# Attention's value product on one Trainium2 core: one fp32 matmul replaced by three products of rounded parts

## The chip, the cores and the metric

The kernel runs on one core of a Trainium2 chip. A core has five engines with a queue of their own each: TensorE (PE in the profile, PEld for its weight loads), VectorE (DVE), ScalarE (ACT), GpSimd (POOL) and SyncE (SP), which here only issues DMA transfers. Each engine takes its instructions strictly in the order in which they were written, and engines wait for one another by semaphores. The metric is the device time of one execution in microseconds (us), from the first to the last instruction. Lower is better.

## What is computed

One layer of a hybrid block over 2048 tokens of width 1024: an input projection, a sparse attention branch, an mLSTM branch, their merge, and a mixture of experts. The change lies in the attention branch, whose last lines in the reference are

```python
logits = jnp.einsum('bqgrd,bqkgd->bqgrk', q_b, k_sel).astype(jnp.float32) * att_scale
logits = jnp.where(valid[:, :, None, None, :], logits, NEG_INF)
p = jax.nn.softmax(logits, axis=-1)
return jnp.einsum('bqgrk,bqkgd->bqgrd', p.astype(v.dtype), v_sel)
```

There are 8 query heads of dimension 64 in two groups (one key and value head for each), and blocks of 128 queries. The kernel does not gather the selected keys: it adds a mask to the scores of all keys that a block may see. The mLSTM recurrence (`mlstm_chunkwise`, 4 heads of dimension 128) is independent of the attention and is computed in the same stage, in between.

## The kernel before

All that follows is about one stage, the function `attend_and_recur`. The stages ahead of it (projection and indexer) and behind it (merge, experts) are not touched.

**Steps.** The stage runs over 32 pairs (n, v), `STEPS`: n is one of 16 query blocks, v one of 2 groups. A pair has n+1 flat steps j, one for each block of 128 keys, 272 flat steps in all, numbered f. All engines walk the same list of flat steps. At each f TensorE computes the transposed scores of 128 keys and 4 heads times 128 queries into `ST` (`logits_t`, L2175 to L2177: two products in the format fp32r and one bf16 product that adds the mask), ScalarE takes the exponential into `PT`, called t_probT (L2342), and TensorE multiplies the values `V`, called t_v, with it into `O`, called t_O (`values`, L2185). This last product has plain fp32 operands. V carries a 65th column of ones, so that row 64 of t_O is the sum of the exponentials. When a pair has ended, ScalarE copies t_O out (L2334).

**The maxima.** The exponential needs each query's maximum. So TensorE also computes the untransposed scores four pairs ahead (`logits`, L2146, into t_L, a ring of 3 buffers), VectorE takes their maxima (L2370), VectorE reduces them at the end of the pair (L2375, t_neg_max), GpSimd makes four diagonal matrices of them (`diagonal`, L2087, t_diag_max), and TensorE turns these into a row (`shift_row`, L2154) that ScalarE copies beside the queries (L2273, t_q_shift).

**The other work.** `side(f)` puts pieces of other work behind the attention's at certain flat steps, on every engine. For 32 units of the causal convolution ScalarE starts (L2297), VectorE adds three taps (L2421), ScalarE takes a tanh (L2303) one flat step later, and VectorE finishes (L2429). For 16 chunks of the mLSTM, one every 15 flat steps from f = 32 on, there are small products on TensorE (t_B), and on VectorE the gates (L2438), t_m_PT, t_m_KW, t_m_Y, a long run of operations on 128x4 elements (L2467 to L2481, the end of it three Newton steps of L2478 to L2480), t_m_T (L2484) and t_m_CN (L2489). GpSimd has three multiplications for a chunk: t_m_QW (L2096), t_m_CN (L2104) and t_m_T (L2110).

**Order.** At flat step f TensorE issues `logits_t(f)`, then `values(f-1)`, then the due `logits` and `side(f)`. `logits_t(f)` waits for the exponential of f-2, since ST has two buffers. `values(f-1)` waits for the exponential of f-1.

```python
                    if before:
                        values(*before)
                    before = (s, j)
```

The ring of t_probT has 3 buffers; the exponential of f waits for `values(f-3)` (`pv_ok`).

## Time and profile before

| what | us |
|---|---|
| median of 3 runs | 3365.78 (3364.29 to 3367.91) |
| span of the profiled execution | 3365.9 |
| the stage, first transposed scores to the last copy-out | about 1204 to 1892 |
| TensorE busy in 1203 to 1893 | 617 of 690 |
| VectorE busy there | 420 |
| ScalarE busy there | 285 |
| GpSimd busy there | 145 |

A matmul's row gives its start and a modelled duration that includes the way through the array, so two rows in a row overlap; how long the array is taken by one is read from the distance of starts. A plain fp32 matmul leaves two rows. Before and behind the stage all engines meet at a barrier, so what the stage wins or loses in length the kernel wins or loses.

### The profile page before, as it was taken

To read this page: it belongs to the slowest core of one execution; us is meant where nothing else is said; L and a number is where in the kernel's file an instruction comes from. 1 tells how busy PE (TensorE), PEld (TensorE's weight loads), DVE (VectorE), ACT (ScalarE), POOL (GpSimd) and SP (SyncE) were. 2 spreads that over 40 slices of the span, in tenths; PEclk is the share of its full clock that TensorE was granted. 3 is DMA by queue.
4 is the path that set the end of the run, shared out by engine and by line. 5 is a ranking of instruction groups with operands and counts; after the bars stand their busy time and mean duration, and the time that the engine had idled before them with its cause. 6 is when DMAs were issued, how large, how long until landed. Compare 5 with 4: busy or idle time off the path is not lost. (4 is left out here: it accounts for less than half of the span.)

```text
span 3365.9 us, 44849 instructions
## 1 busy us (share of the span) xinstructions
PE 3001.8 (89%) x13008; PEld 2234.4 (66%) x13008; DVE 2484.1 (74%) x3912; ACT 1814.6 (54%) x2527; POOL 462.3 (14%) x603
## 2 busy tenths in 40 slices
PE   7998899899899967999989789998499999999990
PEld 5766778678678633555545467887388888888870
DVE  6577589899999965676663445542899999999985
ACT  5322467587678443443434333332477777777770
POOL 0211110100000042221111000000111111111115
PEclk9999999999999978999999899999699999999995
DMA  3222533233212275545423466552478879667868
GB/s 125 88 69 75 146 104 125 92 119 96 65 60 76 67 166 136 116 100 109 92 67 66 125 198 175 170 175 94 188 287 316 319 287 349 243 251 256 310 246 340
DMA packets 382434, 545.93 MB, mean 162 GB/s; under 512 B 36624, under 2 KB 217536, under 8 KB 382160
## 3 DMA queue, kind: packets, MB, share of 16 engines
q1 hardware_dynamic: 349952, 434.02, 41.7%
q0 software_dynamic: 28448, 100.94, 7.9%
q10 hardware_dynamic: 3888, 9.18, 0.7%
q8 instruction: 73, 1.20, 0.1%
q14 instruction: 73, 0.60, 0.1%
HBM read 510.70 MB, written 138.19 MB: 193 GB/s over the span
## 5 line engine op out<-in xcount | busy, mean ns | idle before, releaser
L915 DVE TENSOR_TENSOR e_w_lo<-e_raw,e_w_hi 128x1024 fp32r<-128x1024 f32 x386 | 446.5, 1217 | 2.8 <-ACT e_w_hi L772 2.8
L1585 PE MATMUL x_ps<-h_hi,w_hi 128*128 128x512 f32 (+1 forms) x992 | 391.2, 394 | 5.6 <-PEq L90 4.5
L1585 PE MATMUL x_ps<-h_lo,w_hi 128*128 128x512 f32 (+1 forms) x992 | 389.1, 392 | 0.0
L1585 PE MATMUL x_ps<-h_hi,w_lo 128*128 128x512 f32 (+1 forms) x992 | 389.1, 392 | 0.0
L772 ACT CAST e_w_hi<-e_raw 128x1024 fp32r<-128x1024 f32 x386 | 377.2, 1054 | 4.9 <-PE e_pG L710 4.9
L2370 DVE CUSTOM_DVE_ANT_0 t_junk<-t_L,t_mask 128x512 bf16<-128x512 f32 (+3 forms) x320 | 185.8, 607 | 182.3 <-PE t_L L2146 181.4
L1772 DVE TENSOR_SCALAR_CACHE_REDUCE x_relu<-x_score,x_cand 128x1024 uint8<-128x1024 f32 (+3 forms) x217 | 315.6, 1486 | 3.6
L1687 ACT ACTIVATE x_relu<-x_score,x_cand 128x896 int8<-128x896 f32 (+3 forms) x217 | 281.0, 1296 | 59.8 <-DVE x_cand L1779 59.6
L2185 PE MATMUL t_O<-t_probT,t_v 128*65 128x512 f32 x544 | 292.2, 619 | 20.1 <-ACT t_probT L2342 17.7
L2342 ACT ACTIVATE t_probT<-t_ST 128x512 f32<-128x512 f32 x272 | 160.3, 593 | 276.8 <-PE t_ST L2177 276.2
L710 PE MATMUL e_pG<-e_w_hi,e_x_hi 128*128 128x512 f32 x768 | 246.7, 403 | 3.6 <-DVE e_x_lo L910 3.6
L710 PE MATMUL e_pG<-e_w_lo,e_x_hi 128*128 128x512 f32 x768 | 242.6, 397 | 0.0
L710 PE MATMUL e_pG<-e_w_hi,e_x_lo 128*128 128x512 f32 x768 | 242.1, 396 | 0.0
L2146 PE MATMUL t_L<-t_k,t_q 128*128 128x512 f32 (+3 forms) x320 | 197.1, 664 | 40.9 <-DMA t_q_shift<-q_parts 23.4
L927 DVE TENSOR_TENSOR e_w_lo<-e_raw,e_w_hi 128x1024 fp32r<-128x1024 f32 x192 | 222.4, 1220 | 11.8 <-ACT e_w_hi L785 11.8
L1585 PEld LDWEIGHTS x_ps<-h_hi,w_hi 128*128 128x128 f32 (+1 forms) x992 | 185.8, 187 | 48.3 <-issue 4.9
L1585 PEld LDWEIGHTS x_ps<-h_hi,w_lo 128*128 128x128 f32 (+1 forms) x992 | 185.6, 187 | 42.2
L1585 PEld LDWEIGHTS x_ps<-h_lo,w_hi 128*128 128x128 f32 (+1 forms) x992 | 185.9, 187 | 38.0
L785 ACT CAST e_w_hi<-e_raw 128x1024 fp32r<-128x1024 f32 x192 | 187.5, 1061 | 0.0
L1664 ACT ACTIVATE x_relu<-x_z 128x896 f32<-128x896 f32 (+5 forms) x176 | 141.4, 818 | 66.8 <-DVE x_score L1739 27.8
L710 PEld LDWEIGHTS e_pG<-e_w_lo,e_x_hi 128*128 128x128 f32 x768 | 145.4, 189 | 34.8
L710 PEld LDWEIGHTS e_pG<-e_w_hi,e_x_lo 128*128 128x128 f32 x768 | 145.2, 189 | 34.9
(417 smaller groups left out, 6285.8 us busy)
## 6 DMA issues: line engine op xcount, KB each, us to landing
e_raw<-in_w_exp_gate SPq DMA_DIRECT2D x392, 256.0 KB
e_raw<-in_w_exp_up SPq DMA_DIRECT2D x392, 256.0 KB
e_raw<-in_w_exp_down SPq DMA_DIRECT2D x192, 512.0 KB
projT<-x_out SPq DMA_DIRECT2D x120, 256.0 KB, 3.1
slot_out<-e_y POOLq DMA_DIRECT2D x48, 512.0 KB, 6.2
w_raw<-in_w_in SPq DMA_DIRECT2D x40, 512.0 KB
o_gate<-projT SPq DMA_DIRECT2D x32, 512.0 KB
slot_out<-x_zeros SPq DMA_DIRECT2D x31, 512.0 KB
```

The source lines that it names most:

```text
L710: last = nc.tensor.matmul(psG[:, q, :], x[:, k, :], w[:, k, q * DE:(q + 1) * DE], start=(k == 0 and r == 0), stop=(k == KT - 1 and r == 2))
L772: nc.scalar.copy(w_hi[:, u, :], raw[:, u, :]).then_inc(gh, 1)
L785: nc.scalar.copy(w_hi[:, KT + k, :], raw[:, KT + k, :]).then_inc(dh, 1)
L915: nc.vector.tensor_tensor(w_lo[:, u, :], raw[:, u, :], w_hi[:, u, :].bitcast(F32), ALU.subtract).then_inc(gl, 1)
L927: nc.vector.tensor_tensor(w_lo[:, KT + k, :], raw[:, KT + k, :], w_hi[:, KT + k, :].bitcast(F32), ALU.subtract).then_inc(dl, 1)
L1585: last = nc.tensor.matmul(ps[0:w, u % 4, :], wt[:, m % 2, kk, 0:w], ht[:, kk, q * 512:(q + 1) * 512], start=(kk == 0 and s == 0), stop=(kk ...
L1687: nc.scalar.activation(unused[j][:, 0:width(n)], S[:, j, 0:width(n)], ACT.Sign, bias=cand[:, j:j + 1].bitcast(F32), accum_out=cnt[:, j:j + ...
L1772: last = v.tensor_scalar(unused[j][:, 0:width(n)], S[:, j, 0:width(n)], cand[:, j:j + 1].bitcast(F32), 0.0, ALU.is_ge, ALU.add, accum_out= ...
L2146: nc.tensor.matmul(L[:, made % 3, 0:hi - lo], Q[:, n % 4, h, :], KS[:, v, lo:hi], start=True, stop=True).then_inc(l_ok, 1)
L2185: nc.tensor.matmul(O[0:AD + 1, :, :], V[:, j, v, :], PT[:, (FIRST[s] + j) % 3, :], start=(j == 0), stop=(j == n)).then_inc(pv_ok, 1)
L2342: a.activation(PT[:, f % 3, :], ST[:, u % 2, :], ACT.Exp).then_inc(p_ok, 1)
L2370: v_.tensor_tensor_reduce(junk[:, seen % 3, 0:hi - lo], L[:, seen % 3, 0:hi - lo], MB[:, n % 4, lo:hi], 1.0, -3e38, ALU.add, ALU.max, mxp[ ...
```

## The change

The values V and the exponentials PT are each split in two parts in the format fp32r: a rounded part (a copy by ScalarE, `VH` and `PH`, t_v_hi and t_probT_hi), and what is left (a subtraction, `VL` and `PL`, t_v_lo and t_probT_lo). The value product becomes VH·PH + VL·PH + VH·PL, three fp32r matmuls into the same accumulator. For the values this is done once for each quarter of the keys, by ScalarE and GpSimd. For the exponentials it is done at every flat step: ScalarE copies right behind the exponential, GpSimd subtracts at even flat steps, ahead of its `side(f)`, and VectorE at odd ones, at the start of the next flat step and ahead of that one's maxima. TensorE issues `values` two flat steps behind the scores in place of one. ScalarE's copy-out moves one flat step back. The raw values are loaded in four DMAs of their own.

```diff
@@ gpsimd
+            def probabilities_low(f):
+                pool.wait_ge(ph_ok, f + 1)
+                if f >= 3:
+                    pool.wait_ge(pv_ok, f - 2)
+                g.tensor_tensor(PL[:, f % 3, :], PT[:, f % 3, :], PH[:, f % 3, :].bitcast(F32), ALU.subtract).then_inc(ple_ok, 1)
...
                 for j in range(n + 1):
+                    if (FIRST[s] + j) % 2 == 0:
+                        probabilities_low(FIRST[s] + j)
                     side(FIRST[s] + j)
                 if s + AHEAD < len(STEPS):
                     diagonal(s + AHEAD)
@@ tensor, values
-                pe.wait_ge(p_ok, at_st[s, j] + 1)
+                f = FIRST[s] + j
+                if n == j and j % 4 == 0 and v == 0:
+                    pe.wait_ge(vl_ok, j // 4 + 1)
+                pe.wait_ge(ph_ok, f + 1)
                 if j == 0 and s:
                     pe.wait_ge(ou_ok, s)
-                nc.tensor.matmul(O[0:AD + 1, :, :], V[:, j, v, :], PT[:, (FIRST[s] + j) % 3, :], start=(j == 0), stop=(j == n)).then_inc(pv_ok, 1)
+                nc.tensor.matmul(O[0:AD + 1, :, :], VH[:, j, v, :], PH[:, f % 3, :], start=(j == 0), stop=False)
+                nc.tensor.matmul(O[0:AD, :, :], VL[:, j, v, :], PH[:, f % 3, :], start=False, stop=False)
+                pe.wait_ge(plo_ok if f % 2 else ple_ok, f // 2 + 1)
+                nc.tensor.matmul(O[0:AD + 1, :, :], VH[:, j, v, :], PL[:, f % 3, :], start=False, stop=(j == n)).then_inc(pv_ok, 1)
@@ tensor, loop
-                    if before:
-                        values(*before)
-                    before = (s, j)
+                    if len(before) == 2:
+                        values(*before.pop(0))
+                    before.append((s, j))
@@ scalar
+            def probabilities_high(s, j):
+                f = FIRST[s] + j
+                act.wait_ge(p_ok, at_st[s, j] + 1)
+                if f >= 3:
+                    act.wait_ge(pv_ok, f - 2)
+                a.copy(PH[:, f % 3, :], PT[:, f % 3, :]).then_inc(ph_ok, 1)
...
                     if f >= 3:
-                        act.wait_ge(pv_ok, f - 2)
+                        act.wait_ge(ple_ok if f % 2 else plo_ok, (f - 3) // 2 + 1)
                     a.activation(PT[:, f % 3, :], ST[:, u % 2, :], ACT.Exp).then_inc(p_ok, 1)
                     if j == 0 and s + 1 < len(STEPS):
                         shift_row(s + 1)
-                    if j == 0 and s:
-                        out(s - 1)
+                    probabilities_high(s, j)
+                    if ended(f, 1) is not None:
+                        out(ended(f, 1))
@@ vector (its probabilities_low increments plo_ok)
                 for j in range(n + 1):
+                    if FIRST[s] + j and (FIRST[s] + j) % 2 == 0:
+                        probabilities_low(FIRST[s] + j - 1)
                     while x < due(s, j):
                         maximum(s + AHEAD, x, seen)
```

Line numbers of the changed kernel differ: the value products are L2214, L2215 and L2217 there, the subtractions L2110 (GpSimd) and L2425 (VectorE), the maxima L2418.

TensorE, in the 20th pair (n = 9, v = 1), two flat steps in a row before the change:

```order
L2146 MATMUL t_L<-t_k,t_q 128x512
L2175 MATMUL t_ST<-t_q,t_k 128x512
L2176 MATMUL t_ST<-t_ident_b,t_mask 128x512
L2177 MATMUL t_ST<-t_q_shift,t_k_shift 128x512
L2185 MATMUL t_O<-t_probT,t_v 65x512
L2146 MATMUL t_L<-t_k,t_q 128x512
```

and now:

```order
L2174 MATMUL t_L<-t_k,t_q 128x512
L2201 MATMUL t_ST<-t_q,t_k 128x512
L2202 MATMUL t_ST<-t_ident_b,t_mask 128x512
L2203 MATMUL t_ST<-t_q_shift,t_k_shift 128x512
L2214 MATMUL t_O<-t_probT_hi,t_v_hi 65x512
L2215 MATMUL t_O<-t_probT_hi,t_v_lo 64x512
L2217 MATMUL t_O<-t_probT_lo,t_v_hi 65x512
L2174 MATMUL t_L<-t_k,t_q 128x512
```

The one value product has become three in the same place, and they belong to the flat step before the one that stood there.

VectorE, at flat steps 101 to 104, from t_m_T of a chunk on, before the change (the rows of 128x1 are the second half of a maximum):

```order
L2484 TENSOR_TENSOR t_m_T<-t_m_N,t_m_sc 128x512
L2370 ISA t_junk,t_max_part<-t_L,t_mask 128x512
L2370 ISA t_max_part 128x1
L2421 SCALAR_TENSOR_TENSOR t_v_Y<-t_v_U,t_v_w,t_v_Y 128x512 x3
L2489 TENSOR_TENSOR t_m_CN<-t_m_CN,t_B 128x516
L2370 ISA t_junk,t_max_part<-t_L,t_mask 128x512
L2370 ISA t_max_part 128x1
L2438 SCALAR_TENSOR_TENSOR t_m_AR<-t_m_MN,t_g_cols,t_m_caus 128x128 x4
```

and now:

```order
L2538 TENSOR_TENSOR t_m_T<-t_m_N,t_m_sc 128x512
L2425 TENSOR_TENSOR t_probT_lo<-t_probT,t_probT_hi 128x512
L2418 ISA t_junk,t_max_part<-t_L,t_mask 128x512
L2418 ISA t_max_part 128x1
L2475 SCALAR_TENSOR_TENSOR t_v_Y<-t_v_U,t_v_w,t_v_Y 128x512 x3
L2543 TENSOR_TENSOR t_m_CN<-t_m_CN,t_B 128x516
L2418 ISA t_junk,t_max_part<-t_L,t_mask 128x512
L2418 ISA t_max_part 128x1
L2492 SCALAR_TENSOR_TENSOR t_m_AR<-t_m_MN,t_g_cols,t_m_caus 128x128 x4
L2425 TENSOR_TENSOR t_probT_lo<-t_probT,t_probT_hi 128x512
```

A subtraction stands ahead of the maximum that leads to the taps, and another behind the gates.

GpSimd, around the end of a pair in the second half of the stage, before the change:

```order
L2096 TENSOR_TENSOR t_m_QW<-t_m_X,t_m_WI 128x512
L2110 TENSOR_TENSOR t_m_T<-t_m_T,t_m_gain 128x512
L2087 TENSOR_SCALAR t_diag_max<-t_ident,t_neg_max 128x128 x4
L2104 TENSOR_TENSOR t_m_CN<-t_m_CN,t_m_DEC 128x516
L2096 TENSOR_TENSOR t_m_QW<-t_m_X,t_m_WI 128x512
```

and now:

```order
L2120 TENSOR_TENSOR t_m_QW<-t_m_X,t_m_WI 128x512
L2134 TENSOR_TENSOR t_m_T<-t_m_T,t_m_gain 128x512
L2110 TENSOR_TENSOR t_probT_lo<-t_probT,t_probT_hi 128x512
L2099 TENSOR_SCALAR t_diag_max<-t_ident,t_neg_max 128x128 x4
L2110 TENSOR_TENSOR t_probT_lo<-t_probT,t_probT_hi 128x512 x4
L2128 TENSOR_TENSOR t_m_CN<-t_m_CN,t_m_DEC 128x516
```

The diagonals now have subtractions behind them that TensorE waits for two flat steps later.

## Rows read from the trace of the kernel before

**Rows 1.** Busy us by stretch: PE PEld DVE ACT POOL, granted clock, DMA

```profile
1204.00:1264.00 60.00, 52.95 (x168) 26.59 (x168) 53.66 (x162) 36.68 (x64) 28.82 (x41) 0.91 0.66 157
1264.00:1768.00 504.00, 443.26 (x1740) 243.95 (x1740) 326.17 (x948) 196.15 (x348) 98.78 (x117) 0.94 0.46 104
1768.00:1892.00 124.00, 120.19 (x498) 63.14 (x496) 39.06 (x116) 51.32 (x94) 16.07 (x16) 1.00 0.27 52
```

**Rows 2.** Waits in 1264 to 1768: us in total, times, longest us

```profile
ACT t_v_T L2303 <- DVE t_v_Y L2421: 49.6, 24, 5.1
...
PE t_ST L2175 <- ACT t_probT L2342: 18.3, 2, 14.6
PE t_O L2185 <- ACT t_probT L2342: 17.5, 10, 3.3
...
PE t_L L2146 <- DVE t_max_part L2370: 14.1, 10, 3.9
```

**Rows 3.** Timeline: start, us, instruction, [idle before]; one step, one shift_row

```profile
1701.49 1.02 PE L2185 MATMUL t_O<-t_probT,t_v 128*65 128x512 f32 x2
...
1701.92 0.19 PEld L2146 LDWEIGHTS t_L<-t_k,t_q 128*128 128x128 f32 x1 [0.29 <-issue]
1701.95 0.79 PE L2146 MATMUL t_L<-t_k,t_q 128*128 128x512 f32 x1
...
1702.58 0.40 PE L2175 MATMUL t_ST<-t_q,t_k 128*128 128x512 f32 x1
...
1511.20 0.40 PE L2154 MATMUL t_ST<-t_diag_max,t_to_row 128*128 128x512 f32 x1
...
1511.44 1.02 PE L2185 MATMUL t_O<-t_probT,t_v 128*65 128x512 f32 x2
```

**Rows 4.** Timeline of TensorE in the projection, fp32r matmuls back to back

```profile
599.80 0.39 PE L1585 MATMUL x_ps<-h_lo,w_hi 128*128 128x512 f32 x1
...
601.84 0.39 PE L1585 MATMUL x_ps<-h_lo,w_hi 128*128 128x512 f32 x1
```

**Rows 5.** Groups by line: shapes, count | busy us, mean ns | idle before

```profile
L2096 POOL TENSOR_TENSOR t_m_QW<-t_m_X,t_m_WI 128x512 f32<-128x512 f32 x16 | 20.8, 1299 | 91.1 <-DMA t_m_WI<-inter_rows 91.1
...
L924 DVE TENSOR_TENSOR e_h_lo<-e_pH,e_h_hi 128x512 fp32r<-128x512 f32 x27 | 18.7, 691 | 8.6 <-ACT e_h_hi L782 8.6
...
L782 ACT CAST e_h_hi<-e_pH 128x512 fp32r<-128x512 f32 x27 | 16.0, 592 | 0.0
```

**Rows 6.** Busy by stretch: one late stretch; sum of six; sum of three even

```profile
1487.00:1505.00 18.00, 14.45 (x55) 7.12 (x54) 15.45 (x46) 6.96 (x13) 4.43 (x6) 1.00 0.29 89
...
sum 118.00, PE 98.27 PEld 49.26 DVE 83.44 ACT 41.15 POOL 26.54; mean PE 16.38 PEld 8.21 DVE 13.91 ACT 6.86 POOL 4.42
...
sum 52.00, PE 51.29 PEld 29.95 DVE 33.98 ACT 24.57 POOL 8.63; mean PE 17.10 PEld 9.98 DVE 11.33 ACT 8.19 POOL 2.88
```

**Rows 7.** Timeline of the late stretch: GpSimd and VectorE at once, taps, tanh

```profile
1491.55 1.28 POOL L2096 TENSOR_TENSOR t_m_QW<-t_m_X,t_m_WI 128x512 f32<-128x512 f32 x1 [2.67 <-DMA t_m_WI<-inter_rows]
...
1491.59 1.25 DVE L2480 SCALAR_TENSOR_TENSOR t_m_rs<-t_m_nw,t_m_rs 128x4 f32<-128x4 f32 x1
...
1494.44 1.28 POOL L2110 TENSOR_TENSOR t_m_T<-t_m_T,t_m_gain 128x512 f32<-128x512 f32 x1 [1.61 <-DVE t_m_T L2484]
...
1494.89 2.95 DVE L2421 SCALAR_TENSOR_TENSOR t_v_Y<-t_v_U,t_v_w,t_v_Y 128x512 f32<-128x512 f32 x3
...
1497.87 0.63 ACT L2303 ACTIVATE t_v_T<-t_v_Y 128x512 f32<-128x512 f32 x1 [4.78 <-DVE t_v_Y L2421]
...
1499.04 0.64 PE L2185 MATMUL t_O<-t_probT,t_v 128*65 128x512 f32 x1 [2.77 <-ACT t_probT L2342]
```

**Rows 8.** Durations of one line each: ns min/median/max

```profile
L2480 DVE SCALAR_TENSOR_TENSOR t_m_rs<-t_m_nw,t_m_rs x48: 161/163/1253, 1331.0 to 1883.7; 128x4 f32<-128x4 f32 x48
...
L2421 DVE SCALAR_TENSOR_TENSOR t_v_Y<-t_v_U,t_v_w,t_v_Y x96: 734/752/1803, 1214.7 to 1723.0; 128x512 f32<-128x512 f32 x96
```

**Rows 9.** Timeline at the end of a pair: GpSimd, TensorE

```profile
1569.96 2.88 POOL L2087 TENSOR_SCALAR t_diag_max<-t_ident,t_neg_max 128x128 fp32r<-128x128 f32 x4 [8.66 <-DVE t_neg_max L2375]
...
1570.45 0.40 PE L2175 MATMUL t_ST<-t_q,t_k 128*128 128x512 f32 x1
```

More of the change, by code:

```diff
@@ L2261, in _ @@
                     side(FIRST[s] + j)
-            values(*before)
+            for at in before:
+                values(*at)
             for f in range(FLAT, FLAT + 20):
```

47 lines of the change are left out of this document (37 added, 10 removed).

## The prediction, made before the change was run

> **What bounds the kernel now.** I read the busy table by stretch first, to see which engine fills which part of the stage [rows 1], then the waits of the middle part [rows 2], then the timeline of an undisturbed flat step and of a disturbed one [rows 3, 7]. The stage falls into a head (1204 to 1264, some 20 flat steps, everything busy), a middle (1264 to 1768, 188 steps) and a tail (1768 to 1892, 62 steps, in which no maxima are left). In the tail TensorE is busy 120 of 124 us: it alone is the bound. In the middle it is busy 443 of 504 us and VectorE 326 of 504. TensorE's 61 us of idle time there are mostly waits on ScalarE's exponential (18.3 and 17.5) and on VectorE's maxima (14.1) [rows 2]. One of 14.6 us is a single one, at the start of the mLSTM's first chunk, and the change does not reach it. The others begin at VectorE: in the late stretch shown, the taps of a convolution unit run late, ScalarE waits 4.78 us for them with its tanh, the next exponential stands behind the tanh in ScalarE's queue, and TensorE waits 2.77 us [rows 7]. So the middle alternates. In even stretches (three that I read: 1471 to 1487, 1585 to 1604, 1663 to 1680) TensorE is busy 51.3 of 52 us. In late stretches (six: 1413 to 1431, 1449 to 1471, 1487 to 1505, 1567 to 1585, 1604 to 1626, 1643 to 1663) it is busy 98 of 118 us and VectorE sets the pace [rows 6]; the one shown has VectorE busy 15.45 of 18 us. The six hold 42 flat steps, about 7 each. They come with the run of small operations of each chunk, for 12 chunks of the middle: 84 of the 188 steps.
>
> **TensorE's part.** In an undisturbed step the value product starts at 1701.49 and the product two places on at 1702.58; between them lies one fp32r product of 512 columns [rows 3]. Nine fp32r products back to back take 601.84 - 599.80 = 2.04 us, 0.227 each [rows 4]. So the fp32 product holds the array for 1.09 - 0.227 = 0.86 us. Three fp32r products hold it for 0.68. The change saves 0.18 us for each flat step in which TensorE is the bound. In the tail that is 62 x 0.18 = 11 us, in the even steps of the middle 104 x 0.18 = 19 us: **-30**. In the head and in the late stretches I count nothing, for there TensorE waits anyway. The Trainium skill, FP8 and Floating Point Precision, section TensorE Precision Notes, says that a true fp32 product takes four passes through the array. Four times the measured 0.227 would be 0.91, the saving 0.23 a step and this term -38; the trace shows a little less than four passes, and its number is used.
>
> **ScalarE's part.** Each step gets a copy of 128x512 to fp32r, 0.59 us [rows 5], so exponential and copy take about 1.2 us. TensorE's shortest step is now 3 + 3 products of 0.227, 1.36 us. ScalarE was busy 196 of 504 us in the middle and gets 188 x 0.59 = 111 more: 307 of 504. In the tail it gets 37 on 51 of 124. It stays below the others; I cost it at nothing, and the cover is TensorE's step. If TensorE's step fell under 1.2 us plus ScalarE's side work, it would become the bound. The four copies of the values cost 4 x 0.6 us in the same cover.
>
> **VectorE's part.** One subtraction of 128x512 at every second step, 0.69 us [rows 5]. In the late stretches 84 / 2 = 42 of them, 29 us. They stand ahead of the maxima, on the chain that leads through the taps to tanh, exponential and TensorE. In the even stretches they fit in VectorE's idle time (34.0 busy of 52 us), and in the tail too (39 of 124).
>
> **GpSimd's part, first: what it does to VectorE.** A subtraction of 128x512 costs GpSimd about 1.28 us; its multiplication of that shape has a mean of 1.30 [rows 5]. The trace shows that the two engines stop each other. GpSimd's multiplication ran from 1491.55 to 1492.83, and the operation on 128x4 elements that VectorE began at 1491.59 took 1.25 us, ending with it [rows 7]; the median of that line is 0.163 [rows 8]. The three taps at 1494.89 took 2.95 us beside another one, where three times the median of 0.752 are 2.26 [rows 7, 8]: 0.69 more. So a meeting costs VectorE 0.7 to 1.1 us, say 0.9. GpSimd adds 42 subtractions in the late stretches. About half of VectorE's time there goes to operations with two inputs from SBUF (taps, gates, the small ones, the subtractions themselves), so I count half of them as meetings: 21 x 0.9 = 19 us, between 0 and 42 x 1.1 = 46. The Trainium skill, SBUF — State Buffer, section SBUF: two separate sides, says that a GpSimd operation and a VectorE operation with two SBUF inputs lock each other out for the whole instruction. By that rule the trace agrees: 1.25 us against 0.163.
>
> Together VectorE's late stretches grow by 29 + 19 = 48 us. Laid by hand over the stretch at 1487 to 1505 it comes out the same: two subtractions ahead of the taps (1.4), two meetings with GpSimd (1.4), then one more subtraction and about one meeting, 4 us in all, for 12 stretches 48. VectorE is idle for 29% of the six stretches [rows 6], mostly while TensorE catches up, so a little is absorbed where the unit falls elsewhere: **+44**.
>
> **GpSimd's part, second: its lateness.** At the end of each pair GpSimd builds four diagonals, 2.4 to 2.9 us, as soon as the maxima are there. The next even subtraction stands behind them in its queue, and TensorE wants that one 1.1 us after it has begun the scores two steps later. At 1569.96 the diagonals take 2.88 us, so the subtraction would be ready at 1572.84 + 1.28 = 1574.1, while TensorE has begun the scores in question at 1570.45 and wants it at 1571.6: 2.6 us late [rows 9]. Done so for all 28 pairs against the old times, 12 are late, 10 us in all; part of that falls together with other waits: **+8**. Behind GpSimd's subtraction its chunk multiplications are queued, and VectorE's t_m_CN waits for one of them; they come a step later than before, which the spacing of the chunk's pieces covers.
>
> **The ends.** GpSimd splits the first values between the first diagonals and the setup, 1.3 us, and behind the last exponential come a copy, a subtraction and a product in a row where one product was: **+3**.
>
> **Two steps behind.** While TensorE waits for an exponential it can now run the product of a step earlier. Ten waits at the value product, 17.5 us together [rows 2], are each cut by at most that product and the score product behind it, 0.9 us: **-9**, and the rest of each moves to the scores, which wait for the same exponential.
>
> **The sum.** -30 + 44 + 8 + 3 - 9 = +16 us on the profiled 3365.9, so 3382. The median of the runs, 3365.8, is the same number for this purpose.
>
> **Rivals.**
> (A) *TensorE stays the bound and VectorE absorbs it all.* For it: VectorE is idle for 178 of 504 us in the middle, and the additions, 65 us of subtractions there and some meetings, fit by their sum. Then 250 steps save 0.18 each, -45.5, with +8 + 3 and perhaps the -9: 3322 to 3331; where half of the late stretches absorb, up to 3359. Against it: that idle time lies mostly outside the late stretches. 33%.
> (B) *The two errors meet*, within 0.2% of now (3359 to 3372.5): 14%.
> (C) *The lock on the ports decides; slower.* Each of the 94 even subtractions in the middle meets a VectorE operation, 94 x 0.9 = 85 us. VectorE would need 326 + 65 + 85 = 476 of 504 us. TensorE now fills 88% of the middle; if VectorE can fill no more, the middle becomes 541 us, +37, less 11 in the tail, plus 11 for lateness and ends: 3403, and 3440 if the two queues of three buffers hold each other up besides. It decides from the point where VectorE needs more than 443 us, 88% of 504. By the skill's rule just named, every one of the operations can collide. 11%.
> (D) *Three products don't take less than the old one.* The third has a wait of its own ahead of it, and weight loads behind a wait show 0.29 us of idle and 0.19 us of load [rows 3], 0.48 against 0.227. Then a step costs 0.25 us more, 166 steps 41 us: 3423. Against it: the row of maxima waits too, and the value product starts 0.24 us behind it, no gap [rows 3]. 4%.
> My forecast with its neighbours (3372.5 to 3403) has 38%.
>
> **How the numbers follow.** About 0.2%, 7 us, is what a measurement of this kernel can tell from no change. Faster than that is A, 0.33; the same is B, 0.14; slower are the forecast, C and D, 0.53. The likeliest case alone runs from 3373 to 3403. The range of 8 in 10 leaves out the best part of A (below 3328) and the worst of C and D (above 3425).
>
> **What would show it.** Right: value products at a distance of 0.227 us; a tail shorter by about 11 us; VectorE's median for the subtraction near 0.69 and its mean, and that of the taps, well above their medians; more time in the waits of ScalarE's tanh on the taps; TensorE waiting at L2217 for a subtraction, at pair ends for GpSimd's. Wrong: a middle shorter than 504 us with VectorE's late stretches no longer than now (A), a distance of value products of 0.4 us (D), ScalarE as the engine waited for though not waiting itself, or a single long wait on one of the new value loads.

## The result and the profile after

The changed kernel takes 3436.03 us (median, 3432.31 to 3437.26); beside it the kernel before takes 3366.85 (3364.29 to 3369.38). The ratio is 1.0198, with an interval from 1.0183 to 1.0213. So the change costs 69 us where +16 was forecast, and lies outside the range of 3328 to 3425. The profiled execution spans 3433.7 us, 67.8 more than that of before, with a granted TensorE clock of 0.940 in place of 0.950. One execution of a later run (gp_reads_one) took 9651 us; it is left out of that run's median.

The stage holds 65 of these 68 us. I cut it, here and below, at the starts of the scores of flat steps 20 and 210, which stand at 1260 and 1768 in the kernel before, and end it at the start of the last copy-out:

| kernel | head | middle | tail | stage |
|---|---|---|---|---|
| before | 55.6 | 508.5 | 123.4 | 687.6 |
| after | 63.1 | 552.5 | 137.3 | 752.9 |

The busy table of after by stretch, which answers to [rows 1]; its columns are the same, PE, PEld, DVE, ACT and POOL busy, then the clock:

```profile
1204.00:1266.00 62.00, 48.09 (x171) 28.23 (x171) 57.73 (x156) 45.90 (x79) 46.61 (x53) 0.86 0.54 138
1266.00:1819.00 553.00, 435.42 (x1945) 284.56 (x1943) 429.39 (x1061) 314.46 (x546) 237.16 (x215) 0.90 0.39 95
1819.00:1957.00 138.00, 119.29 (x562) 76.06 (x561) 68.77 (x146) 88.58 (x156) 56.72 (x47) 0.91 0.19 47
```

In the middle TensorE is busy 435 us where it was 443, but it now idles for 118 of 553 us, before for 61 of 504. VectorE rose from 326 to 429, GpSimd from 99 to 237, ScalarE from 196 to 314. In the tail TensorE, busy for 120 of 124 us before, idles for 19 us of 138, and its granted clock fell from 1.00 to 0.91.

TensorE's waits over the whole stage, which answer to those of TensorE in [rows 2] (total, times, longest), and ScalarE's on the taps and the next line of the middle:

```profile
PE t_O L2217 <- DVE t_probT_lo L2425: 96.8, 36, 6.7
PE t_ST L2201 <- ACT t_probT L2387: 19.3, 5, 13.2
PE t_B L2248 <- DVE t_m_Y L2509: 13.1, 9, 3.9
PE t_L L2174 <- DVE t_max_part L2418: 8.9, 5, 3.4
PE t_O L2214 <- ACT t_out L2378: 7.6, 13, 1.5
PE t_O L2217 <- POOL t_probT_lo L2110: 3.3, 5, 1.2
```

```profile
ACT t_v_T L2336 <- DVE t_v_Y L2475: 60.4, 24, 6.9
ACT t_m_AR L2340 <- DVE t_m_AR L2492: 38.1, 12, 10.9
```

Two thirds of TensorE's waiting in the stage, 100 of 150 us, stand at one instruction, the third value product (L2217), and it is VectorE's subtraction that is late, at the odd steps; GpSimd's is waited for in 3.3 us. The rows read as a plain story: move subtractions away from VectorE, or give them more time. Both were tried (lag3, table) and neither is the cure.

Two things came as forecast. The value products start 0.24, 0.23 and 0.22 us apart, beside the 1.09 of [rows 3]:

```profile
1839.08 0.40 PE L2214 MATMUL t_O<-t_probT_hi,t_v_hi 128*65 128x512 f32 x1
1839.32 0.39 PE L2215 MATMUL t_O<-t_probT_hi,t_v_lo 128*64 128x512 f32 x1
1839.55 0.39 PE L2217 MATMUL t_O<-t_probT_lo,t_v_hi 128*65 128x512 f32 x1
1839.77 0.40 PE L2201 MATMUL t_ST<-t_q,t_k 128*128 128x512 f32 x1
```

And the prices of [rows 5] held. The groups of the new operations, of the page and by line for VectorE (count | busy us, mean ns | idle time before):

```profile
L2110 POOL TENSOR_TENSOR t_probT_lo<-t_probT,t_probT_hi 128x512 fp32r<-128x512 f32 x136 | 181.8, 1337 | 327.3 <-ACT t_probT_hi L2372 317.6
...
L2372 ACT CAST t_probT_hi<-t_probT 128x512 fp32r<-128x512 f32 x272 | 168.5, 620 | 8.4
```

```profile
L2425 DVE TENSOR_TENSOR t_probT_lo<-t_probT,t_probT_hi 128x512 fp32r<-128x512 f32 x136 | 107.8, 793 | 52.7 <-ACT t_probT_hi L2372 47.9 <-PE t_O L2217 4.1 <-issue 0.3
```

VectorE's median for it is 0.687 us, its mean 0.793, its longest 1.833. What stands between median and mean is the subject of most of the experiments.

GpSimd and VectorE in the tail, answering to [rows 7]: three operations of GpSimd, what VectorE began beside each, and what followed:

```profile
1842.99 1.27 POOL L2110 TENSOR_TENSOR t_probT_lo<-t_probT,t_probT_hi 128x512 fp32r<-128x512 f32 x1 [3.28 <-ACT t_probT_hi L2372]
1843.02 1.27 DVE L2525 TENSOR_TENSOR t_m_ms<-t_m_ms,t_m_rec 128x4 f32<-128x4 f32 x1
...
1845.66 1.27 POOL L2110 TENSOR_TENSOR t_probT_lo<-t_probT,t_probT_hi 128x512 fp32r<-128x512 f32 x1 [1.40 <-ACT t_probT_hi L2372]
1845.72 1.23 DVE L2533 TENSOR_TENSOR t_m_nw<-t_m_nw,t_m_ms 128x4 f32<-128x4 f32 x1
...
1847.35 1.26 POOL L2120 TENSOR_TENSOR t_m_QW<-t_m_X,t_m_WI 128x512 f32<-128x512 f32 x1 [0.41 <-DMA t_m_WI<-inter_rows]
1847.38 1.24 DVE L2533 TENSOR_TENSOR t_m_nw<-t_m_nw,t_m_ms 128x4 f32<-128x4 f32 x1
...
1849.66 0.68 DVE L2425 TENSOR_TENSOR t_probT_lo<-t_probT,t_probT_hi 128x512 fp32r<-128x512 f32 x1
...
1850.40 0.69 PE L2217 MATMUL t_O<-t_probT_lo,t_v_hi 128*65 128x512 f32 x1 [4.25 <-DVE t_probT_lo L2425]
```

Three operations on 128x4 elements, 0.16 us each when undisturbed, take 1.23 to 1.27 us and end with GpSimd's. That is 3.3 us lost inside eight, in a chain of small steps at whose end stands the subtraction; TensorE waits 4.25 us for it. The third of GpSimd's operations, t_m_QW, is chunk work that the kernel before has too; there only such work could do this in the tail, and now one more operation comes with every second step.

Counted over the whole stage of after: 50 operations of VectorE lasted over 0.3 us longer than undisturbed beside a subtraction of GpSimd, together 45.0 us (3 in the head, 38 in the middle, 9 in the tail). Undisturbed means here and below the lower quartile of the same operation in the run dve_all, in which GpSimd subtracts nothing of the exponentials. Of the 38, 18 fall in the late stretches of the prediction (16.0 us). The operations that were never stretched are as telling: of 224 maxima over 128x512, which read the scores from PSUM, the memory that TensorE writes to, 54 began beside such a subtraction, and the longest of all took 0.693 us for a usual 0.69.

### The profile page after: what moved, and what is told of

It is laid out like the page before. It is cut to its first block and busy times, and to the rows that moved or that the text cites. A ratio compares the mean times of both kernels' runs of the same rounds, so it can differ in the third digit from the quotient of the medians.

```text
span 3433.7 us, 46483 instructions
## 1 busy us (share of the span) xinstructions
PE 2985.3 (87%) x13279; PEld 2288.0 (67%) x13280; DVE 2620.8 (76%) x4048; ACT 1980.9 (58%) x2803; POOL 659.5 (19%) x743
## 5 line engine op out<-in xcount | busy, mean ns | idle before, releaser
L2418 DVE CUSTOM_DVE_ANT_0 t_junk<-t_L,t_mask 128x512 bf16<-128x512 f32 (+3 forms) x320 | 186.3, 606 | 123.0 <-PE t_L L2174 122.0
L2110 POOL TENSOR_TENSOR t_probT_lo<-t_probT,t_probT_hi 128x512 fp32r<-128x512 f32 x136 | 181.8, 1337 | 327.3 <-ACT t_probT_hi L2372 317.6
L2217 PE MATMUL t_O<-t_probT_lo,t_v_hi 128*65 128x512 f32 x272 | 118.6, 436 | 100.6 <-DVE t_probT_lo L2425 96.8
L2372 ACT CAST t_probT_hi<-t_probT 128x512 fp32r<-128x512 f32 x272 | 168.5, 620 | 8.4
L2203 PE MATMUL t_ST<-t_q_shift,t_k_shift 65*128 65x512 f32 x272 | 172.6, 635 | 0.0
```

The costliest lines, as they stand in the source:

```text
L2110: g.tensor_tensor(PL[:, f % 3, :], PT[:, f % 3, :], PH[:, f % 3, :].bitcast(F32), ALU.subtract).then_inc(ple_ok, 1)
L2203: nc.tensor.matmul(o, K2[0:AD + 1, v, keys], Q2[0:AD + 1, n % 4, v * R4:(v + 1) * R4, :], start=False, stop=True).then_inc(st_ok, 1)
L2418: v_.tensor_tensor_reduce(junk[:, seen % 3, 0:hi - lo], L[:, seen % 3, 0:hi - lo], MB[:, n % 4, lo:hi], 1.0, -3e38, ALU.add, ALU.max, mxp[ ...
```

## The experiments

Each kernel ran beside the kernel before; their medians there were 3364.5 to 3367.1. Three causes stood against each other: **lateness** (a subtraction comes too late for its product, and more time would cure it), **the lock** (GpSimd's subtraction stops VectorE), and **plain work** on engines whose cover I had taken for granted, VectorE's subtractions and ScalarE's copies.

**1. The new work without the new products.** The kernel before, with ScalarE's copy and both kinds of subtraction put in, and the exponential waiting until its buffer's low part is written; TensorE reads neither part.

```
@@ ScalarE, each step (split_unread, against the kernel before)
+                        act.wait_ge(ple_ok if f % 2 else plo_ok, (f - 3) // 2 + 1)
                     a.activation(PT[:, f % 3, :], ST[:, u % 2, :], ACT.Exp).then_inc(p_ok, 1)
...
+                    probabilities_high(s, j)
@@ GpSimd, even steps (VectorE at odd ones)
+                g.tensor_tensor(PL[:, f % 3, :], PT[:, f % 3, :], PH[:, f % 3, :].bitcast(F32), ALU.subtract).then_inc(ple_ok, 1)
```

> The kernel before with its one fp32 value product one step behind, but ScalarE also makes the rounded copy of each step's exponentials and GpSimd and VectorE subtract in turn, as in the changed kernel; TensorE reads neither. (The split of the values is left out. The exponential of f+3 still waits for the subtraction of f, as in the changed kernel.) Theory 1, lateness: what costs in the changed kernel is that TensorE waits in the middle of each value product for a subtraction that stands behind VectorE's chunk work; then this kernel, where the subtraction may be some two steps later without anyone waiting, is at 3375 to 3400. Theory 2, work: the added operations and the lock between GpSimd and VectorE cost by themselves; then it is at 3420 to 3460.

Measured: 3446.51 us, ratio 1.0235 (1.0218 to 1.0253), 79 us over before, though TensorE never waits for a subtraction directly. The damage does not need the third product's wait. VectorE's operations stretched beside GpSimd's subtractions are 54 here, 45.9 us, as many as in after.

**2. The new products without the subtractions.** In no_low the copies stay and the third product reads the rounded part again. In products_only the exponential is written in fp32r at once, so the copies are gone too.

```
@@ TensorE (no_low, against after)
-                pe.wait_ge(plo_ok if f % 2 else ple_ok, f // 2 + 1)
-                nc.tensor.matmul(O[0:AD + 1, :, :], VH[:, j, v, :], PL[:, f % 3, :], start=False, stop=(j == n)).then_inc(pv_ok, 1)
+                nc.tensor.matmul(O[0:AD + 1, :, :], VH[:, j, v, :], PH[:, f % PR, :], start=False, stop=(j == n)).then_inc(pv_ok, 1)
@@ ScalarE (products_only, against no_low; all three products read PT)
-        PT = sb("probT", [P, PR, 512])
+        PT = sb("probT", [P, PR, 512], F32R)
...
-                    probabilities_high(s, j)
```

> The changed kernel with no subtraction of the exponentials on GpSimd or VectorE; the third value product reads the rounded part again in place of the rest. ScalarE's copies, the three products and the distance of two steps stay. (It leaves out the low part of the exponentials.) If the three products save what I worked out and ScalarE's copies are covered: 3315 to 3345. If ScalarE's copies are what makes the changed kernel slow (theory 3): above 3390. If three products do not take less of TensorE than the fp32 one: 3360 or more.

> As the kernel without subtractions (no_low), but ScalarE's rounded copy is left out as well: the exponential is written in fp32r at once, and all three value products read it, two steps behind. (It leaves out the low part of the exponentials.) no_low had gained nothing on the kernel before. Theory S, ScalarE's copies give back what the three products save: 3325 to 3340, that is 26 to 41 us under no_low. Theory P, three products do not free TensorE: 3360 to 3370.

Measured: no_low 3366.51, ratio 0.9997 (0.9988 to 1.0007); products_only 3341.45, ratio 0.9921 (0.9899 to 0.9943). So three products and two steps of distance bring 26 us, and 272 copies on an engine that is busy for less than half of the stage take 25 of them back. The subtractions cost the remaining 70 us. The time of no_low is the one that the third theory of its expectation names, and products_only shows that its reason is not the right one: the three products do take less.

**3. The copies alone.** The kernel before, with only ScalarE's copy added behind each exponential; nothing reads it.

```
@@ ScalarE (copy_unread, against the kernel before)
+                    probabilities_high(s, j)
```

> The kernel before with its fp32 product one step behind, and ScalarE makes the rounded copy of each step's exponentials, which nobody reads. Nothing on GpSimd or VectorE is added. Theory S: the copies cost by themselves, 3385 to 3400. If the copies cost only in a kernel whose TensorE step has become short: 3366 to 3375.

Measured: 3380.0, ratio 1.0041 (1.0029 to 1.0052). In the kernel before the copies cost 13 us, between the two ranges expected: not nothing, and not the 25 of experiment 2. The edit puts the copy ahead of ScalarE's copy-out at the end of a pair, and TensorE's waits for the copy-out show it, in the kernel before and then in copy_unread:

```profile
PE t_O L2185 <- ACT t_out L2334: 2.1, 6, 0.4
```

```profile
PE t_O L2190 <- ACT t_out L2344: 15.6, 23, 1.0
```

They grew by 13.5 us, and TensorE's other waits in the stage did not grow to speak of. So the 13 us here are, as far as the waits tell, the order in ScalarE's queue and not the copies' own time. The next run changes that order.

**4. The copy-out ahead of the copy.** In the changed kernel ScalarE copies a finished pair's output out of PSUM behind that step's rounded copy, and TensorE's first product of the next pair waits for it.

```
@@ ScalarE (no_low_out_first; the same edit makes dve_all_out_first of dve_all)
+                    if ended(f, LAG - 1) is not None:
+                        out(ended(f, LAG - 1))
                     probabilities_high(s, j)
-                    if ended(f, LAG - 1) is not None:
-                        out(ended(f, LAG - 1))
```

> As no_low (three products, ScalarE's copies, no subtraction of the exponentials), but at a pair's end ScalarE copies the output out ahead of the rounded copy in place of behind it. In no_low TensorE waited 12.7 us in all for the copy-out (15 times), in products_only 3.5. If part of the 25 us that the rounded copies cost is this: 3355 to 3362. If the cost is only that ScalarE comes back late behind its own waits: 3364 to 3369.

Measured: 3353.97, ratio 0.9965 (0.9953 to 0.9977), 12.5 us less than no_low (11.4 if each is taken from the kernel before beside it). TensorE's waits for the copy-out in no_low, and then in no_low_out_first:

```profile
PE t_O L2218 <- ACT t_out L2381: 12.7, 15, 2.0
```

```profile
PE t_O L2218 <- ACT t_out L2381: 4.9, 7, 1.3
```

So about half of the copies' price of 25 us is a matter of order in ScalarE's queue. The rest, 12.5 us between this run and products_only, belongs to the copies themselves; where it arises no run here shows, and by the stages of the two profiled executions it is 5.7 us and the order 16.5. Experiment 3 is no second measurement of it, since there all 13 us can be the order.

**5. GpSimd's operation without its reading.** GpSimd's subtraction becomes a memset of the same tile (0.52 us, no input); all waits and VectorE's subtractions stay. A memset is shorter than a subtraction, so in gp_writes_long a memset of a spare tile stands ahead of it.

```
@@ GpSimd (gp_writes, against after)
-                g.tensor_tensor(PL[:, f % 3, :], PT[:, f % 3, :], PH[:, f % 3, :].bitcast(F32), ALU.subtract).then_inc(ple_ok, 1)
+                g.memset(PL[:, f % PR, :].bitcast(F32), 0.0).then_inc(ple_ok, 1)
@@ GpSimd (gp_writes_long, against gp_writes: ahead of it)
+                g.memset(PAD[:, :], 0.0)
```

> The changed kernel, but GpSimd's subtraction at the even steps is replaced by a memset of the same tile, which reads nothing from SBUF and is shorter. (It leaves out the low part of the even steps.) VectorE's subtractions stay. TensorE waited only 8 us at even steps in the changed kernel, so what this run saves beyond 8 us is the lock of GpSimd against VectorE. Theory 1 (lateness of VectorE's subtraction, the lock a smaller part of it): 3395 to 3420. Theory of the lock (my rival C): 3375 or less. If the lock costs nothing on the path: 3425 or more.

> As gp_writes, but GpSimd writes a spare tile first and then the low part, two memsets that together hold it for about 1.05 to 1.3 us, as long as its subtraction, without reading SBUF. (It leaves out the low part of the even steps.) gp_writes was 46 us under the changed kernel. Theory of the lock (the reading blocks VectorE): 3388 to 3400, as gp_writes. Theory of GpSimd's lateness (its length counts): 3420 to 3436.

Measured: 3389.59 and 3389.48, ratios 1.0068 (1.0051 to 1.0085) and 1.0074 (1.0052 to 1.0096). The first lies between the ranges of the two theories, nearer to that of lateness; the second decides between them, in the lock's favour. 0.52 more us of GpSimd at each even step cost nothing; at 1.05 us the two memsets are still 0.3 us shorter than a subtraction. With writes alone, GpSimd's share of the change costs nothing that shows, and 46.5 us of the loss are gone. The busy table of the whole stage, after and gp_writes_long:

```profile
1204.00:1957.00 753.00, 602.80 (x2675) 388.85 (x2674) 555.89 (x1361) 448.95 (x780) 340.49 (x313) 0.90 0.36 90
```

```profile
1204.00:1912.00 708.00, 583.00 (x2668) 377.91 (x2667) 511.14 (x1357) 446.02 (x776) 290.86 (x443) 0.92 0.39 95
```

VectorE executes the same instructions (1361 and 1357 records) in 555.9 and in 511.1 us. These 45 us are the lock, by VectorE's own busy time, and the kernel's time differs by 46.5. The single meetings counted in after give the same 45.0 us; in neither of these two runs is a like operation with two inputs held up by a memset alone.

**6. How much of the reading matters.** gp_reads_one is gp_writes_long with the second memset made a copy of PT: one input instead of none.

```
@@ GpSimd (gp_reads_one, against gp_writes_long)
                 g.memset(PAD[:, :], 0.0)
-                g.memset(PL[:, f % PR, :].bitcast(F32), 0.0).then_inc(ple_ok, 1)
+                g.tensor_copy(PL[:, f % PR, :], PT[:, f % PR, :]).then_inc(ple_ok, 1)
```

> As gp_writes_long, but the second of GpSimd's two operations at the even steps is a copy of the exponentials, which reads one tile from SBUF, in place of a memset. (It leaves out the low part of the even steps and puts the exponentials in its place.) The whole stays about 1.1 to 1.3 us long, of which the reading part is about 0.6. If any reading on GpSimd blocks VectorE for its length: 46 us times 0.6 / 1.28, so 3405 to 3415. If it takes the two inputs of the subtraction: 3386 to 3394, as gp_writes_long.

Measured: 3400.08 (three executions), ratio 1.0109 (1.0089 to 1.0129), between the two ranges expected. GpSimd's groups in gp_reads_one:

```profile
L2120 POOL CAST t_probT_lo<-t_probT 128x512 fp32r<-128x512 f32 x136 | 92.5, 680 | 0.0
...
L2119 POOL MEMSET t_pad<- 128x512 f32 x136 | 71.3, 524 | 324.5 <-ACT t_probT_hi L2382 320.5 <-PE t_O L2227 3.8
```

0.68 us of reading at each even step cost 11 us (13 if each run is taken from the kernel before beside it), the 1.34 of the subtraction 46. The meetings can be seen in the means. The taps, which the change does not touch, in gp_writes_long, gp_reads_one and after (the median is 752 ns in all three, as in [rows 8]):

```profile
L2485 DVE SCALAR_TENSOR_TENSOR t_v_Y<-t_v_U,t_v_w,t_v_Y 128x512 f32<-128x512 f32 x96 | 76.7, 799 | 11.8 <-ACT t_v_Y L2340 9.5
```

```profile
L2485 DVE SCALAR_TENSOR_TENSOR t_v_Y<-t_v_U,t_v_w,t_v_Y 128x512 f32<-128x512 f32 x96 | 78.2, 814 | 13.0 <-ACT t_v_Y L2340 10.7
```

```profile
L2475 DVE SCALAR_TENSOR_TENSOR t_v_Y<-t_v_U,t_v_w,t_v_Y 128x512 f32<-128x512 f32 x96 | 86.2, 898 | 12.6 <-ACT t_v_Y L2330 10.3
```

799, 814 and 898 ns. VectorE's own subtractions go 717, 746, 793 (medians 686 or 687). Summed over all of VectorE's operations of the stage, the time beyond the median of their line and shape is 24, 37 and 73.5 us in these three, and 70 in split_unread. Twice the length costs about four times the price. The count of meetings says how: 16 operations of VectorE were stretched beside the copy, by 0.38 us on average, and 50 beside the subtraction, by 0.90. Part of the difference in number may be that the copy comes 0.52 us later than the subtraction would, behind the spare memset; no run here separates that from the number of inputs.

**7. All subtractions on VectorE.** GpSimd is relieved, VectorE has 136 more operations; then the same with the copy-out ahead.

```
@@ (dve_all, against after)
     def gp(f):
+        return False
@@ GpSimd and VectorE
-                    if (FIRST[s] + j) % 2 == 0:
+                    if gp(FIRST[s] + j):
                         probabilities_low(FIRST[s] + j)
```

> The changed kernel with all subtractions of the exponentials on VectorE, none on GpSimd. VectorE's 136 subtractions with no reading partner on GpSimd cost 23 us (gp_writes against no_low). Theory of the lock: 136 more cost as much or somewhat more as VectorE fills up, 23 to 40, and the 46 us of the lock go: 3412 to 3430, under the changed kernel's 3436. Theory that GpSimd's share was a relief for VectorE: 3440 or more.

> As dve_all (all subtractions on VectorE), with ScalarE's copy-out ahead of its rounded copy at a pair's end. It computes what the changed kernel computes. In no_low this order saved 12 us. If TensorE's wait for the copy-out is a cost of its own here too: 3388 to 3396. If VectorE's subtractions hide it (TensorE waits for those anyway): 3399 to 3406. The kernel before, 3366, stays faster in either case.

Measured: 3402.37, ratio 1.0112 (1.0094 to 1.0131), and 3396.05, ratio 1.0092 (1.0075 to 1.0109). The kernel is 34 us faster than after, with 136 subtractions moved onto the engine that was already waited for, and below the 3412 to 3430 of the lock's theory: the second 136 subtractions on VectorE cost 14 us over gp_writes_long, where the first 136 cost 23. The two runs of this pair can hardly be told apart, since their intervals overlap. TensorE's largest wait in dve_all:

```profile
PE t_O L2223 <- DVE t_probT_lo L2431: 99.9, 52, 14.4
```

The same wait, 99.9 us for 96.8, in a kernel that is 34 us shorter. The row says where TensorE waits, not what the wait costs.

**8. More distance.** The value product three steps behind the scores, with four buffers for both parts (the diagonals give up two of theirs for the room).

```
@@ (lag3, against after)
-    AHEAD, RING = 4, 6
+    AHEAD, RING, DRING = 4, 6, 4
...
+    PR, LAG = 4, 3
```

> The changed kernel with the value products three steps behind the scores in place of two, four buffers of each part, and four buffers of the diagonals in place of six to make room. Nothing else moves. Theory 1: each wait for a subtraction shrinks by one flat step, about 1.6 us; of the 41 waits, 100 us in all, about half go: 3380 to 3400. Theory 2: TensorE only waits elsewhere, at the maxima or at the exponential: 3425 to 3440.

Measured: 3429.82, ratio 1.0182 (1.0165 to 1.0199), 6 us less than after. Its waits of TensorE:

```profile
PE t_L L2180 <- DVE t_max_part L2424: 41.1, 23, 5.1
PE t_ST L2207 <- ACT t_probT L2393: 31.2, 14, 16.0
PE t_O L2223 <- DVE t_probT_lo L2431: 29.9, 15, 4.7
...
PE t_O L2220 <- ACT t_out L2384: 15.8, 14, 7.9
```

The wait at the subtraction went from 96.8 to 29.9 us, 67 less, and most of it came back: 32 at the maxima, 12 at the exponential, 8 at the copy-out. By parts of the stage the middle is 15 us shorter than in after, and head and tail are 5 and 3 us longer. The smaller ring of the diagonals is not what gives it back: GpSimd waits for the maxima ahead of them as in after (54.3 us for 53.8) and not for a free buffer. So lateness is at most a small part of the loss: VectorE's queue is late as a whole, and any first product that needs it shows the wait.

**9. Another share-out.** GpSimd also takes the odd subtractions in the four flat steps of each chunk in which VectorE was latest.

```
@@ (table, against after)
+        return f % 2 == 0 or (f >= CHUNK0 and (f - CHUNK0) % PERIOD in (8, 9, 10, 11))
```

> The changed kernel with another division of the subtractions: GpSimd takes the even steps and besides those 8 to 11 steps behind a chunk's first (some 30 more), where VectorE's long run stands; VectorE takes the rest. In the changed kernel TensorE waited some 75 us for just these of VectorE's. Theory 1 (waiting in the queue): 3380 to 3400. Theory of VectorE's time and the lock: each subtraction moved saves VectorE 0.7 us and costs it up to 1.2 by the lock: 3425 to 3450.

Measured: 3445.16, ratio 1.0228 (1.0207 to 1.025), 9 us more than after. What VectorE is spared in subtractions, it loses in stops: 32 subtractions fewer are 22 us, but 79 of its operations are stretched beside GpSimd's where 50 were, by 70.0 us in place of 45.0, and it is busy for 563 us of the stage for 556. TensorE now also waits 17.6 us for GpSimd's subtractions, 3.3 in after.

**10. The gain in its parts.** lag2_fp32 is the kernel before with its one fp32 value product two steps behind, nothing else. two_products is products_only with the third product taken out, and the low part of the values given a column of zeros so that its product spans all 65 rows.

```
@@ TensorE (lag2_fp32, against the kernel before)
-                    if before:
-                        values(*before)
-                    before = (s, j)
+                    if len(before) == 2:
+                        values(*before.pop(0))
+                    before.append((s, j))
@@ TensorE (two_products, against products_only)
-                nc.tensor.matmul(O[0:AD, :, :], VL[:, j, v, :], PT[:, f % PR, :], start=False, stop=False)
-                nc.tensor.matmul(O[0:AD + 1, :, :], VH[:, j, v, :], PT[:, f % PR, :], start=False, stop=(j == n)).then_inc(pv_ok, 1)
+                nc.tensor.matmul(O[0:AD + 1, :, :], VL[:, j, v, :], PT[:, f % PR, :], start=False, stop=(j == n)).then_inc(pv_ok, 1)
```

> The kernel before with one edit: the fp32 value product is issued two flat steps behind the scores in place of one, and ScalarE's copy-out one flat step later. It computes exactly what the kernel before does. My term for this was -9: 3355 to 3361. If the waits only move to the scores: 3364 to 3370. If the later copy-out costs: above 3370.

> As products_only (the exponential written in fp32r, no copy, no subtraction), with two value products, of the rounded values and of their rest. (It leaves out the low part of the exponentials.) Against products_only it takes 0.227 us from each of the flat steps in which TensorE is the bound. If that is still so in some 166 of 272 steps: 3341 - 38 = 3303. If VectorE has become the bound of the middle and TensorE that of the tail alone (62 steps): about 3327.

Measured: lag2_fp32 3358.55, ratio 0.9987 (0.9974 to 1.0), at the edge of what can be told from no change: its medians say -7 us, its ratio -4. two_products 3332.02, ratio 0.9904 (0.9884 to 0.9923), only 9 us less than products_only, though 272 products of 0.23 us are gone, 62 us. TensorE is no longer what a step waits for, not even in the tail, which the 3327 of the expectation still left to it. The tail shows what takes its place. TensorE and the others there, in products_only and in two_products:

```profile
1745.00:1867.00 122.00, 111.14 (x554) 72.72 (x554) 38.92 (x112) 52.03 (x94) 15.57 (x15) 0.97 0.32 54
```

```profile
1734.00:1857.00 123.00, 103.92 (x491) 69.37 (x491) 38.73 (x112) 52.04 (x94) 15.45 (x15) 0.89 0.27 53
```

TensorE's busy time falls from 120 (before) to 111 and 104 us, and the tail stays at 122 to 123 us. ScalarE in products_only at one of four such places, then TensorE:

```profile
1745.34 0.63 ACT L2343 ACTIVATE t_m_AR<-t_m_AR 128x512 f32<-128x512 f32 x1 [3.32 <-DVE t_m_AR L2494]
1745.88 0.61 ACT L2345 ACTIVATE t_m_X<-t_m_X 128x512 f32<-128x512 f32 x1
1746.40 0.58 ACT L2390 ACTIVATE t_probT<-t_ST 128x512 fp32r<-128x512 f32 x1
```

```profile
1747.03 0.50 PE L2205 MATMUL t_ST<-t_q,t_k 128*128 128x512 f32 x1 [2.86 <-ACT t_probT L2390]
```

ScalarE stands for 3.32 us at the mLSTM's decay (L2343), which VectorE delivers late; the attention's exponential is behind it, and TensorE waits 2.86 us. There are four of these in the tail. In the kernel before ScalarE waits there for 5.0 us in all, in products_only for 10.9. TensorE's waits for the exponential in the tail grew by 6.8 us, so most of the 9 us that its products saved came back as waiting; that it is this chain that holds them is read from the rows.

## The sum of the parts

From the medians, each line one edit further, with differences taken from each kernel's distance to the kernel before beside it:

| step | kernel | us | difference |
|---|---|---|---|
| kernel before | before | 3367 | |
| value product two steps behind | lag2_fp32 | 3359 | -7 |
| three fp32r products for one fp32 | products_only | 3341 | -18 |
| ScalarE's 272 copies | no_low | 3367 | +25 |
| VectorE's 136 subtractions (GpSimd only writes) | gp_writes_long | 3389 | +23 |
| GpSimd's 136 subtractions read | after | 3436 | +47 |

The split of the first 26 us into 7 and 18 is loose, since lag2_fp32 is hardly clear of no change; their sum is not. A second way round agrees: in the kernel before, copies cost 13; with 23 and 46 added to them 3449 is expected, and split_unread has 3446.5. So the prices of the two kinds of subtraction hardly depend on which products TensorE makes. No kernel here that splits the product and keeps the low part of the exponentials beats the kernel before; the nearest is dve_all_out_first with 3396. no_low_out_first, products_only and two_products do, and they leave it out.

By parts of the stage, in the profiled executions:

| kernel | head | middle | tail | stage |
|---|---|---|---|---|
| products_only | 57.1 | 484.2 | 121.8 | 663.2 |
| no_low | 58.7 | 504.0 | 122.7 | 685.4 |
| gp_writes_long | 60.4 | 519.9 | 127.5 | 707.7 |
| after | 63.1 | 552.5 | 137.3 | 752.9 |

## Why the prediction was wrong

The side was right and the size was not: +16 forecast, +69 measured. Three steps failed. The lock was priced for the late stretches alone, at +19, and costs +46 over the whole stage. ScalarE's copies were put at nothing, as covered by TensorE's step, and cost +25. And the tail, "it alone is the bound", was to give back 11 us and gave 1.6. Term by term:

**TensorE, -30, and two steps behind, -9.** Measured -26 together (products_only), some -4 to -7 of it for the distance. The saving of 0.18 us a step is real, the spacing of the products shows it. The part that failed is the tail: "it alone is the bound". From 120 of 124 busy I read that any faster product would shorten it, 11 us. It shortened by 1.6. TensorE's busy time fell by 9 us there, and its waits for the exponential rose from 2.4 to 9.2, behind ScalarE's wait for VectorE's decay. That this chain holds the tail is read from the trace; no run here shortened it. A share of 97% says which engine is the bound now, not by how much. The middle gave 24 us, what -19 and some of -9 had foreseen.

**ScalarE, 0.** Measured +25. Here the cover was named, but only by its length: 1.2 us of exponential and copy in a step of 1.36. No rival had a price for it either. About half of it, 12.5 us, was the copy-out behind the copy, which the order of ScalarE's queue shows before any run: I counted what stands behind the new operation in GpSimd's queue (the chunk multiplications), and not in ScalarE's. The sentence "if TensorE's step fell under 1.2 us plus ScalarE's side work, it would become the bound" may be the right condition for the other half: ScalarE's other work (tanh, decay, copy-outs) comes in bunches with the chunks, and there each copy lengthens a queue for which TensorE waits. That is argued and not shown, and I did not work out in how many steps it holds.

**VectorE's own subtractions, +29.** Measured +23 for all 136, where I had counted 42 in full and the rest at nothing. That the size is near is partly luck: from no_low to gp_writes_long the middle grew by 16 us where 29 were forecast, and the head (1.7) and the tail (4.8), where I let all fit, made up some of the rest.

**The lock, +19 (0 to 46).** Measured +46, the largest miss. The mechanism and the price of one meeting, 0.7 to 1.1 us, were right: the 50 meetings counted in after cost 0.90 each. Even their number in the late stretches of the middle was, 18 for 21, and 16.0 us for 19. What failed is that I counted no others: in the run all 136 subtractions are candidates, and 32 meetings fall elsewhere, 20 in the rest of the middle (9 of them in the flat step just ahead of a late stretch), 9 in the tail and 3 in the head. The tail alone, in which I saw VectorE idle for two thirds of the time and expected none that matter, grew by 9.8 us from gp_writes_long to after, for there VectorE's chain of small steps is what ScalarE and TensorE come to wait for. Rival C had more meetings than there were, 94 in the middle for 38, but the right mechanism, and its time, 3403 to 3440, holds the result. That is partly luck: it lengthened the middle by 37 us (44 measured) and shortened the tail by 11, which grew by 14. I had given it 11%, and made it depend on VectorE needing more than 443 of 504 us. It had no need of that: VectorE is busy for 429 of 553 us in the middle of after, 78%. An engine that works in bursts for others decides long before it is full. By the Trainium skill's page SBUF — State Buffer, section SBUF: two separate sides, which limits the lock for an operation with two SBUF inputs to "a GpSimd op that reads SBUF", gp_writes_long and after should differ, and they do, 3389.5 to 3436.0; of how much it says nothing.

**GpSimd's lateness, +8.** At even steps the gap between second and third product beyond its usual distance sums to 8.6 us, near the forecast. That they cost the kernel 8 us is not shown: TensorE's waits for GpSimd are 3.3 us, and in gp_writes_long 0.52 us more of GpSimd cost nothing. At odd steps the gap is 105 us, VectorE's, which no term named. It deserved none: with the stops taken away it shrinks (67.3 us of waits in gp_writes_long), and cured by itself it returns 6 us of 67 (lag3). It is where the other terms become visible.

**The ends, +3.** The head grew by 7.5 us, of which 1.5 are there in products_only and the rest came with copies (1.6), subtractions (1.7) and lock (2.7). I had counted no lock, no copies and no VectorE work in the head, where everything was busy; that was a reason to count in full.

**Rivals.** A fell: the middle grew, its late stretches with it. D fell with the spacing of 0.23 us; TensorE's waits there are for the data. C was right in kind. Had the sum taken the lock's upper end (46), the copies at their measured price (+25) and the tail at nothing for TensorE, it would have been 16 + 27 + 25 + 11 = +79, and +73 with VectorE's own work at 23 for 29; +69 was measured.

## What to carry over

Before you give GpSimd an operation that reads SBUF (the memory from which the engines take their operands), find out where VectorE is waited for, and count its possible stops over the whole stage and not only where VectorE is busiest, however idle the two are by their shares (here 50 of 136 met one, 0.90 us each); if the work can be VectorE's, it may be cheaper on the busier engine (here by 34 us). Cover is not the idle share of an engine but what stands behind the new operation in its own queue at the moments when someone waits for that queue. And where most of TensorE's waiting stands at one line, shift that wait by one edit before you believe it is the cost.

## What the runs showed of the hardware

A small operation that the lock catches ends with GpSimd's: in the tail's rows above 128x4 elements took 1.23 to 1.27 us beside a GpSimd operation with two inputs, 0.16 alone. It does not catch everything: the maxima, which read PSUM, never took longer. 136 GpSimd memsets of 128x512 cost the kernel nothing measurable; one small operation of VectorE with a single int32 input (t_m_rs<-t_m_ms, 128x4) was nevertheless held up eight times in gp_writes_long, 0.45 to 1.08 us for 0.17, 4 us in all. A GpSimd copy with one input, 0.68 us, cost about a quarter of what the subtraction with two, 1.34 us, cost (11 to 46 us for 136).

A wait of TensorE costs more than its length. Behind the wait of 4.25 us in the tail of after, its rows read:

```profile
1851.32 0.65 PE L2202 MATMUL t_ST<-t_ident_b,t_mask 128*128 128x512 bf16 x1
...
1852.19 0.63 PE L2214 MATMUL t_O<-t_probT_hi,t_v_hi 128*65 128x512 f32 x1
1852.62 0.63 PE L2215 MATMUL t_O<-t_probT_hi,t_v_lo 128*64 128x512 f32 x1
1853.05 0.63 PE L2217 MATMUL t_O<-t_probT_lo,t_v_hi 128*65 128x512 f32 x1
```

The products start 0.43 us apart, against 0.23 in the rows at 1839: the lower of the two clocks, 1.2 for 2.4 GHz. The granted clock of this stretch, 1849.4 to 1856.1, is 0.50. The tail's granted clock, 1.00 before, is 0.97 in products_only, 0.91 in after and 0.89 in two_products, where TensorE has the least to do. There the missing products should have left it busy for 120 - 62 x (0.86 - 0.45) = 95 us, and it shows 104: part of what a lighter TensorE saves is lost in speed, behind four waits for the exponential, 17.9 us together.
